# Hybrid decoder step: state updates by pairs of banks, scores on 32x32 blocks, sample updates behind their outputs

## The chip, the cores and the metric

The kernel runs on one core of a Trainium2 chip, written for the engines PE (TensorE), DVE (VectorE), ACT (ScalarE), POOL (GpSimd) and SP (which issues most DMAs). The metric is the device time of one execution in microseconds; smaller is better.

## The reference

The reference computes one step of a two-layer decoder for a prompt of 512 tokens and 8 samples of 8 tokens. In each layer half of the width is attention in three branches, and the other half a gated recurrence (HGRN2) with 4 heads and a 128 x 128 state per head, which is what the change is about. It is computed in chunks of 32 tokens for the prompt, and of 8 tokens for each sample:

```
a = where(causal, einsum('bnhcd,bnhsd->bnhcs', qe, ke), 0)   # scores within a chunk
o_intra = einsum('bnhcs,bnhse->bnhce', a, vh)
def step(S, inp):                                            # over the chunks
    qe_n, kd_n, v_n, dec_n = inp
    o_n = einsum('bhcd,bhde->bhce', qe_n, S)
    S = dec_n[..., None] * S + einsum('bhcd,bhce->bhde', kd_n, v_n)
    return S, o_n
o = rms_norm(o_intra + o_inter, out_gain) * sigmoid(g)
```

Everything is float32. All outputs of the layer feed one projection and an MLP.

## The kernel before

One program walks through the two layers. A layer has four parts: projections, then a block with the recurrence and the prompt's attention, then the compressed keys and the samples' attention, then output projection and MLP. Within a part each engine has its own list of instructions, written out by hand, and the engines wait for each other on semaphores. An engine works its list in order, so what stands behind a wait waits too. The order of the work around the change is the order of the calls at the end of each engine's function (L1332 to L1378 for PE, L1413 to L1457 for ACT, L1529 to L1575 for DVE).

The recurrence handles the prompt in four tiles t of 128 tokens, each of four chunks of 32, and the samples in two halves s of two heads. For a tile of the prompt:

- `scores` (L1171) makes the 128 x 128 scores of each head in bank 0 with four full products (L1178), though only the four 32 x 32 blocks on the diagonal are needed, and transposes the decayed keys into bank 1 (L1181). DVE's `masked` (L1466) copies what the mask lets through into `aTm`; the rest stays zero. ACT's `keep_kd` (L1381) copies the keys to `kdt`.
- `updates` (L1184) makes keys times values for the four chunks j into banks 4 to 7, one bank for a chunk, 32 rows of the array for each (L1191). It begins when the state update before it (`hg_state`) is done.
- `states` (L1479) is DVE's chain: for each chunk and head one instruction of 128 x 128 (L1489) computes the next state from the one before and the bank, 16 in all.
- `intra` (L1205) and `inter` (L1220) add scores times values and queries times states into bank 2 (bank 6 for the last tile). ACT's `keep_outputs` (L1388) norms the result into `on`, `turn_outputs` (L1250) transposes it into bank 3 (7), and DVE's `finish` (L1522) gates it.

The samples have `sample_outputs` (L1229, bank 3), `sample_updates` (L1195, again banks 4 to 7) and DVE's `sample_states` (L1496), which can overwrite the states only once the outputs are made; `select_samples` (L1506) takes the outputs from bank 3. `PROMPT` and `SAMPLES` number the six uses of banks 4 to 7: prompt 0, prompt 1, samples 0, prompt 2, samples 1, prompt 3.

Attention follows in the same block: `turn` (L1310) transposes queries and keys for it, through banks named in `TURN_BANKS`, and ACT copies them (L1429); `att_scores` (L1261) makes scores into banks 0 and 1, then 2 and 3, in turn (L1274), and DVE adds the mask and takes the maximum (L1561, L1563). The second `att_scores` uses banks 2 and 3 and waits for four of the finishes.

## Time and profile before

| | us |
|---|---|
| median of 3 runs | 1946.52 (1944.40 to 1946.86) |
| the profiled execution's own time | 1949.37 |
| its span, from first to last instruction | 1947.6 |
| PE, DVE, ACT, POOL busy in the span | 1862.8, 1139.6, 785.7, 665.2 |
| mean granted clock of PE | 0.985 |

In the rows further down, a line such as L1191 is that of this kernel. A product (matmul) of float32 appears as two records of PE, so x32 are 16 products. Shapes of PE are rows*columns of the weights and rows x columns of the moving operand. `HT`, `R`, `OT` and `RAW` are the large buffers of which all named tiles are cut.

### The profile page before, as it was taken

How to read it: one execution, taken by the hardware profiler on the slowest of the kernel's cores; microseconds unless marked ns; L12 is line 12 of the kernel's file. 1: busy time of each engine (PE TensorE's matmuls, PEld its weight loads, DVE VectorE, ACT ScalarE, POOL GpSimd, SP SyncE). 2: the span in 40 equal slices, each digit the busy share in tenths (PEclk: the TensorE clock that was granted, in tenths of full speed). 3: DMA queues.
4: the chain of work that ended last, by engine and by line, in shares of the span. 5: the costliest groups of instructions: out<-in, count | busy, mean ns of one | idle time of the engine just before them, and what ended most of it. 6: DMA issues, size and time to landing. Idle time of an engine off the chain costs nothing. (4 is left out here: it accounts for less than half of the span.)

```text
span 1947.6 us, 36998 instructions
## 1 busy us (share of the span) xinstructions
PE 1862.8 (96%) x15057; PEld 1720.0 (88%) x15057; DVE 1139.6 (59%) x1847; ACT 785.7 (40%) x1543; POOL 665.2 (34%) x452
## 2 busy tenths in 40 slices
PE   7999899999899999999999998999988999999999
PEld 6988567997799999999989875679968999999998
DVE  5588776555445454555537878756454455545554
ACT  4564375444433131313146635745444422323131
POOL 2432545230233333333323334544103333333331
PEclk8999999999999999999999998999999999999999
DMA  4221521325422222222222224222462222222221
GB/s 163 87 67 44 172 67 55 91 87 162 122 87 84 77 79 87 87 87 78 75 76 74 72 69 134 66 86 70 134 167 74 87 87 78 76 86 87 87 81 55
DMA packets 196053, 175.68 MB, mean 90 GB/s; under 512 B 11388, under 2 KB 189358, under 8 KB 195758
## 3 DMA queue, kind: packets, MB, share of 16 engines
q1 hardware_dynamic: 195778, 173.30, 29.2%
q8 instruction: 120, 1.97, 0.4%
q14 instruction: 47, 0.39, 0.1%
q10 hardware_dynamic: 108, 0.03, 0.0%
HBM read 162.67 MB, written 10.62 MB: 89 GB/s over the span
## 5 line engine op out<-in xcount | busy, mean ns | idle before, releaser
L389 POOL TENSOR_TENSOR WX<-RAW,WX 128x2048 fp32r<-128x2048 f32 (+1 forms) x46 | 210.7, 4581 | 357.6 <-ACT WX L385 357.6
L2661 DVE TENSOR_TENSOR sq<-sq 128x288 f32<-128x288 f32 x128 | 156.7, 1229 | 198.2 <-ACT sq L2626 198.2
L389 POOL TENSOR_TENSOR m_wl<-RAW,m_wh 128x2048 fp32r<-128x2048 f32 x36 | 165.1, 4587 | 308.5 <-ACT m_wh L385 308.5
L399 PE MATMUL bank<-UH,m_wh 128*128 128x288 f32 x640 | 188.9, 295 | 0.0
L401 PE MATMUL bank<-UH,m_wl 128*128 128x288 f32 x640 | 188.9, 295 | 0.0
L400 PE MATMUL bank<-UL,m_wh 128*128 128x288 f32 x640 | 188.7, 295 | 0.0
L401 PE MATMUL bank<-UH,WX 128*128 128x288 f32 x576 | 170.6, 296 | 0.0
L399 PE MATMUL bank<-UH,WX 128*128 128x288 f32 x576 | 170.6, 296 | 0.0
L400 PE MATMUL bank<-UL,WX 128*128 128x288 f32 x576 | 170.5, 296 | 0.0
L2680 DVE TENSOR_TENSOR OT<-bank,rstd 128x288 f32<-128x288 f32 x128 | 58.2, 454 | 186.3 <-PE bank L401 186.3
L2683 DVE TENSOR_TENSOR XT<-XT,OT 128x288 f32<-128x288 f32 x128 | 157.1, 1227 | 4.4
L1839 PE MATMUL bank<-FTS,W1S 128*128 128x256 f32 (+1 forms) x512 | 156.5, 306 | 0.0
L399 PE MATMUL bank<-m_ah,m_wh 128*128 128x288 f32 x512 | 151.3, 296 | 0.0
L401 PE MATMUL bank<-m_ah,m_wl 128*128 128x288 f32 x512 | 151.1, 295 | 0.0
L400 PE MATMUL bank<-m_al,m_wh 128*128 128x288 f32 x512 | 151.0, 295 | 0.0
L1842 PE MATMUL bank<-FTS,W1S 128*128 128x256 f32 (+1 forms) x512 | 150.7, 294 | 0.0
L1841 PE MATMUL bank<-FTS,W1S 128*128 128x256 f32 (+1 forms) x512 | 150.6, 294 | 0.0
L385 ACT ACTIVATE WX<-RAW 128x2048 fp32r<-128x2048 f32 (+1 forms) x46 | 86.4, 1878 | 157.3 <-PE bank L401 142.3
L2626 ACT ACTIVATE sq<-bank 128x288 f32<-128x288 f32 x128 | 52.5, 410 | 235.6 <-PE bank L401 218.9
L401 PE MATMUL bank<-m_ah,WX 128*128 128x288 f32 x448 | 132.7, 296 | 0.0
L400 PE MATMUL bank<-m_al,WX 128*128 128x288 f32 x448 | 132.6, 296 | 0.0
L399 PE MATMUL bank<-m_ah,WX 128*128 128x288 f32 x448 | 132.5, 296 | 0.0
(396 smaller groups left out, 5324.5 us busy)
## 6 DMA issues: line engine op xcount, KB each, us to landing
RAW<-in_w_up SPq DMA_DIRECT2D x32, 1024.0 KB, 5.4
RAW<-in_w_down SPq DMA_DIRECT2D x32, 1024.0 KB, 5.1
RAW<-in_w_in SPq DMA_DIRECT2D x20, 1024.0 KB, 5.0
R<-in_cache_nsa_kv SPq DMA_DIRECT2D x128, 64.0 KB
HT<-in_cache_nsa_kv SPq DMA_DIRECT2D x128, 64.0 KB, 2.7
RAW<-in_w_in SPq DMA_DIRECT2D x8, 792.0 KB, 4.5
R<-in_cache_nsa_kv SPq DMA_DIRECT2D x48, 128.0 KB, 2.3
out<-R SPq DMA_DIRECT2D x10, 512.0 KB, 4.6
```

What stands on the lines that cost most here:

```text
L385: act.activation(S.granule(S.wh, i, w), S.granule(S.raw, i, w), ACT.Copy).then_inc(sem(S.name + "w_hi"), 1)
L389: eng.tensor_tensor(S.granule(S.wl, i, w), S.granule(S.raw, i, w), S.granule(S.wh, i, w).bitcast(F32), ALU.subtract).then_inc(sem(S.name + ...
L399: pe.matmul(out, wh[:, c, cols], ah[:, c, n], start=(c == 0), stop=False)
L400: pe.matmul(out, wh[:, c, cols], al[:, c, n], start=False, stop=False)
L401: ins = pe.matmul(out, wl[:, c, cols], ah[:, c, n], start=False, stop=(c == KC - 1))
L1839: pe.matmul(out, W1H[:, s, c, cols], xh, start=first and (h == 0 or CU[w][1] == 0), stop=False, skip_group_check=True)
L1841: pe.matmul(out, W1H[:, s, c, cols], xl, start=False, stop=False, skip_group_check=True)
L1842: ins = pe.matmul(out, W1L[:, s, c, cols], xh, start=False, stop=last, skip_group_check=True)
L2626: act.activation(relu[n % 4], bank[2 + u % 6][:, 0:HALF], ACT.Relu).then_inc(sem("m_relued"), 1)
L2661: dve.tensor_tensor(relu[n % 4], relu[n % 4], relu[n % 4], ALU.mult).then_inc(sem("relu_squared"), 1)
L2680: dve.tensor_tensor(grown[n % 2], bank[2 + u % 6][:, 0:HALF], rstd[:, halves(s)], ALU.mult).then_inc(sem("m_added"), 1)
L2683: dve.tensor_tensor(x, x, grown[n % 2], ALU.add).then_inc(sem("m_grown"), 1)
```

## The change

Five edits, all in the block with the recurrence:

- `updates` and `sample_updates` are done by pairs of banks: the products for banks 4 and 5 first, when DVE has done the first half of the update before (`hg_chain`, or `hg_s_chain` for samples), and those for banks 6 and 7 when it has done all of it. `states` and `sample_states` wait for each pair apart.
- Scores of the prompt are made as 16 products of 32 x 32 (4 chunks, 4 heads), packed in 128 columns of bank 0; the mask, `aTm` and DVE's copy shrink to a quarter. `intra` takes them as 16 products of 32 rows by 32 columns, each from row group j into partitions 32j to 32j + 31 of the output bank.
- Sample updates come directly behind the sample outputs on PE, and DVE's sample states before the selection. The last state update comes ahead of `finish_samples`, and `finish(2)` and `turn_outputs(2)` come after attention's first score.
- The normed outputs have two buffers, so that ACT waits for the transposes of two tiles before.
- ACT norms the samples before it keeps the last keys, the turns begin behind the last updates, and the banks of the turns are swapped to fit.

The diff, each line with 12 spaces less at its start:

```diff
@@ -86,7 +86,7 @@
-put("hgmask", (i[:, None] // CH == i[None] // CH) & (i[:, None] <= i[None]))
+put("hgmask", i[:, None] % CH <= np.arange(CH)[None])
@@ -951,8 +951,9 @@
-aTm = [cut(HH * P).rearrange("p (h n) -> p h n", h=HH) for _ in range(2)]
-kdt, on = (cut(HH * P).rearrange("p (h e) -> p h e", h=HH) for _ in range(2))
...
+aTm = [cut(HH * CH).rearrange("p (h n) -> p h n", h=HH) for _ in range(2)]
+kdt, *on = (cut(HH * P).rearrange("p (h e) -> p h e", h=HH) for _ in range(3))
@@ -987,7 +988,7 @@
-TURN_BANKS = (0, 1, 0, 1, 2, 0, 1, 2)
+TURN_BANKS = (1, 0, 2, 1, 0, 2, 1, 2)
@@ -1175,32 +1176,49 @@
-                ins = pe.matmul(s[0:r, h * r:(h + 1) * r], hf[:, h, c], hq[:, h, c], start=True, stop=True)
+                if t == NT:
+                    ins = pe.matmul(s[0:r, h * r:(h + 1) * r], hf[:, h, c], hq[:, h, c], start=True, stop=True)
+                    continue
+                for j in range(NCK):
+                    x = slice(t * P + j * CH, t * P + (j + 1) * CH)
+                    ins = pe.matmul(s[j * CH:(j + 1) * CH, h * CH:(h + 1) * CH], hf[:, h, x], hq[:, h, x],
+                                    start=True, stop=True, skip_group_check=True)
...
+        def room(r, half):
...
+            if r == 0:
+                return
+            if half:
+                pe.wait_ge(sem("hg_state"), r)
+            elif r - 1 in PROMPT:
+                pe.wait_ge(sem("hg_chain"), HH * ((NCK - 1) * PROMPT.index(r - 1) + 2))
+            else:
+                pe.wait_ge(sem("hg_s_chain"), SAMPLES.index(r - 1) + 1)
...
         def updates(t):
-            if t:
-                pe.wait_ge(sem("hg_state"), PROMPT[t])
...
-            for h in range(HH):
-                for j in range(NCK):
-                    rr = slice(j * CH, (j + 1) * CH)
-                    ins = pe.matmul(bank[4 + j][:, h * P:(h + 1) * P], kdt[rr, h, :],
-                                    hi_tok[rr, t, h * P:(h + 1) * P], start=True, stop=True)
-            ins.then_inc(sem("hg_updates"), 1)
+            for half in range(2):
+                room(PROMPT[t], half)
+                for h in range(HH):
+                    for j in (2 * half, 2 * half + 1):
+                        rr = slice(j * CH, (j + 1) * CH)
+                        ins = pe.matmul(bank[4 + j][:, h * P:(h + 1) * P], kdt[rr, h, :],
+                                        hi_tok[rr, t, h * P:(h + 1) * P], start=True, stop=True)
+                ins.then_inc(sem("hg_updates"), 1)
         def sample_updates(s):
-            pe.wait_ge(sem("hg_state"), SAMPLES[s])
...
+                room(SAMPLES[s], h % 2)
...
-            ins.then_inc(sem("hg_updates"), 1)
+                ins.then_inc(sem("hg_updates"), 1)
         def intra(t):
@@ -1213,9 +1231,11 @@
-                pe.matmul(out_of(t)[:, h * P:(h + 1) * P], aTm[t % 2][:, h], hi_tok[:, t, h * P:(h + 1) * P],
-                          start=(h == 0), stop=False, skip_group_check=True)
+                for j in range(NCK):
+                    rr = slice(j * CH, (j + 1) * CH)
...
+                    pe.matmul(out_of(t)[rr, h * P:(h + 1) * P], aTm[t % 2][rr, h], hi_tok[rr, t, h * P:(h + 1) * P],
+                              start=(h == 0), stop=False, skip_group_check=True)
         def inter(t):
@@ -1255,7 +1275,7 @@
-                ins = pe.transpose(turned_of(t)[:, h * P:(h + 1) * P], on[:, h], ident)
+                ins = pe.transpose(turned_of(t)[:, h * P:(h + 1) * P], on[t % 2][:, h], ident)
...
         def att_scores(n):
@@ -1313,8 +1333,8 @@
-                pe.wait_ge(sem("hg_kd_kept" if u else "hg_masked"), NT)
-            elif u == 4:
+                pe.wait_ge(sem("hg_masked" if u else "hg_kd_kept"), NT)
+            elif u == 2:
@@ -1337,27 +1357,26 @@
         updates(1)
         inter(0)
         sample_outputs(0)
+        sample_updates(0)
         scores(2)
         intra(1)
-        sample_updates(0)
         inter(1)
         turn_outputs(0)
         updates(2)
         sample_outputs(1)
+        sample_updates(1)
         intra(2)
         scores(3)
+        inter(2)
         turn_outputs(1)
-        sample_updates(1)
-        inter(2)
+        updates(3)
+        turn(0)
+        turn(1)
         pe.wait_ge(sem("hg_s_normed"), 1)
         pe.wait_ge(sem("hg_finished"), 2)
         for s in range(2):
             ins = pe.transpose(bank[3][:, s * P:(s + 1) * P], s_out[s], ident)
         ins.then_inc(sem("hg_out_turned"), 1)
-        turn(0)
-        turn(1)
-        updates(3)
-        turn_outputs(2)
         for u in range(2, len(TURNS)):
             turn(u)
         for n in range(NA + LAG + 1):
@@ -1366,6 +1385,7 @@
             if n == 0:
                 intra(3)
                 inter(3)
+                turn_outputs(2)
             if n == 1:
                 for t in range(4):
                     turn_plain(t)
@@ -1382,22 +1402,22 @@
         def keep_kd(t):
...
-                act.wait_ge(sem("hg_updates"), PROMPT[t - 1] + 1)
+                act.wait_ge(sem("hg_updates"), 2 * PROMPT[t - 1] + 2)
...
         def keep_outputs(t):
...
-            if t:
...
-                act.wait_ge(sem("hg_out_turned"), t + (t == 3))
+            if t >= 2:
...
+                act.wait_ge(sem("hg_out_turned"), t - 1)
...
-                ins = act.activation(on[:, h], out_of(t)[:, h * P:(h + 1) * P], ACT.Square, accum_out=r[:, h:h + 1])
+                ins = act.activation(on[t % 2][:, h], out_of(t)[:, h * P:(h + 1) * P], ACT.Square, accum_out=r[:, h:h + 1])
...
-                ins = act.activation(on[:, h], out_of(t)[:, h * P:(h + 1) * P], ACT.Copy, scale=r[:, h:h + 1])
+                ins = act.activation(on[t % 2][:, h], out_of(t)[:, h * P:(h + 1) * P], ACT.Copy, scale=r[:, h:h + 1])
...
         def norm_samples():
@@ -1418,10 +1438,10 @@
         keep_outputs(0)
         keep_kd(2)
         keep_outputs(1)
+        norm_samples()
         keep_kd(3)
         act.activation(gate, win_tok[:, :, 256:WINW], ACT.Exp, scale=-1.0).then_inc(sem("gate_exp"), 1)
-        norm_samples()
         keep_outputs(2)
         for u, (k, t) in enumerate(TURNS):
             act.wait_ge(sem("turned"), u + 1)
@@ -1467,8 +1487,8 @@
-            dve.copy_predicated(aTm[t % 2], const("hgmask").bitcast(U32).unsqueeze(1).to_broadcast([P, HH, P]),
-                                bank[0].rearrange("p (h n) -> p h n", h=HH)).then_inc(sem("hg_masked"), 1)
+            dve.copy_predicated(aTm[t % 2], const("hgmask").bitcast(U32).unsqueeze(1).to_broadcast([P, HH, CH]),
+                                bank[0][:, 0:HH * CH].rearrange("p (h n) -> p h n", h=HH)).then_inc(sem("hg_masked"), 1)
         def sample_masked():
@@ -1477,9 +1497,10 @@
         def states(t):
-            dve.wait_ge(sem("hg_updates"), PROMPT[t] + 1)
...
+                if j % 2 == 0:
+                    dve.wait_ge(sem("hg_updates"), 2 * PROMPT[t] + 1 + j // 2)
@@ -1494,13 +1515,15 @@
         def sample_states(s):
-            dve.wait_ge(sem("hg_updates"), SAMPLES[s] + 1)
...
+                dve.wait_ge(sem("hg_updates"), 2 * SAMPLES[s] + 1 + h % 2)
...
+                if h % 2 == 0:
+                    ins.then_inc(sem("hg_s_chain"), 1)
...
         def select_samples(s):
@@ -1531,18 +1554,17 @@
         states(0)
         masked(1)
         states(1)
+        sample_states(0)
         select_samples(0)
         masked(2)
-        sample_states(0)
         finish(0)
         states(2)
         select_samples(1)
+        sample_states(1)
         masked(3)
         finish(1)
-        sample_states(1)
+        states(3)
         finish_samples()
-        states(3)
-        finish(2)
         dve.wait_ge(sem("gate_exp"), 1)
         step(dve, dve.tensor_scalar(gate, gate, 1.0, None, ALU.add), "dve_done")
         dve.reciprocal(gate, gate).then_inc(sem("gate_made"), 1)
@@ -1561,6 +1583,8 @@
+            if n == 0:
+                finish(2)
```

The order of PE, from the third tile's scores (before) to the second tile's inter. The names in brackets are semaphores: `hg_chain` counts DVE's single state instructions, `hg_state` whole updates. Before:

```order
L1178 MATMUL bank<-R_0 128x128 [waits hg_kd_kept_47,hg_masked_49]
L1178 MATMUL bank<-R_0 128x128 x3
L1181 MATMUL bank<-cst,R_0 128x128 x4
L1217 MATMUL bank<-R_0,HT 128x128 [waits hg_out_kept_55,hg_masked_49]
L1217 MATMUL bank<-R_0,HT 128x128 x3
L1202 MATMUL bank<-OT,R_0 128x512 [waits hg_apart_53,hg_s_kd_kept_52,hg_state_32]
L1202 MATMUL bank<-OT,R_0 128x512 x3
L1225 MATMUL bank<-R_0 32x128 [waits hg_state_32]
```

Now, L1220 being the sample updates, L1184 the scores and L1237 intra:

```order
L1220 MATMUL bank<-OT,R_0 128x512 [waits hg_chain_51,hg_apart_54,hg_s_kd_kept_53]
L1220 MATMUL bank<-OT,R_0 128x512
L1220 MATMUL bank<-OT,R_0 128x512 [waits hg_state_32]
L1220 MATMUL bank<-OT,R_0 128x512
L1184 MATMUL bank<-R_0 32x32 [waits hg_kd_kept_47,hg_masked_49]
L1184 MATMUL bank<-R_0 32x32 x15
L1188 MATMUL bank<-cst,R_0 128x128 x4
L1237 MATMUL bank<-R_0,HT 32x128 [waits hg_out_kept_56,hg_masked_49]
L1237 MATMUL bank<-R_0,HT 32x128 x15
L1245 MATMUL bank<-R_0 32x128 [waits hg_state_32]
```

The sample updates moved ahead of scores and intra, and were split in two, the first with a wait on half an update.

PE where attention begins, now (L1294 is an attention score, L1237 and L1245 the last intra and inter):

```order
L1294 MATMUL bank<-R_0 128x512 [waits turn_kept_63]
L1294 MATMUL bank<-R_0 128x512
L1237 MATMUL bank<-R_0,HT 32x128 [waits hg_state_32,hg_masked_49]
L1237 MATMUL bank<-R_0,HT 32x128 x15
L1245 MATMUL bank<-R_0 32x128 [waits hg_state_32]
L1245 MATMUL bank<-R_0 32x128 x15
L1278 MATMUL bank<-cst,HT 128x128 [waits hg_finished_59,hg_out_kept_56]
L1278 MATMUL bank<-cst,HT 128x128 x3
L1294 MATMUL bank<-R_0 128x512 [waits hg_finished_59,turn_kept_63]
```

The two L1278 rows, the transposes of the third tile's outputs, stood ahead of the third to the eighth turn before; they are now between the first and the second score.

## Rows read from the trace of the kernel before

**Rows 1.** The page, part 1: busy us, share of the span, instructions of each engine.
```profile
PE 1862.8 (96%) x15057; PEld 1720.0 (88%) x15057; DVE 1139.6 (59%) x1847; ACT 785.7 (40%) x1543; POOL 665.2 (34%) x452
```
**Rows 2.** DVE's waits, first block, then second: who waited for whom; us in all, times, longest.
```profile
DVE R L1489 <- PE bank L1191: 4.3, 4, 1.5
DVE R L1501 <- PE bank L1202: 3.0, 2, 1.9
...
DVE R L1489 <- PE bank L1191: 3.8, 4, 1.6
DVE R L1501 <- PE bank L1202: 2.0, 2, 1.2
DVE HT L1470 <- PE bank L1178: 1.7, 1, 1.7
```
**Rows 3.** Timeline of DVE, first block: start us, us, instructions, [idle before <-releaser].
```profile
202.39 4.22 DVE L1489 SCALAR_TENSOR_TENSOR R<-R,bank 128x128 f32<-128x128 f32 x16 [0.84 <-PE bank L1191]
...
206.65 0.74 DVE L1470 COPY_PREDICATED HT<-cst,bank 128x512 f32<-128x512 uint32 x1
...
213.07 1.12 DVE L1511 SCALAR_TENSOR_TENSOR rstd<-bank,cst,rstd 128x128 f32<-128x128 f32 x3
...
216.71 4.22 DVE L1501 SCALAR_TENSOR_TENSOR R<-R,bank 128x128 f32<-128x128 f32 x16 [1.87 <-PE bank L1202]
220.85 0.74 DVE L1526 SCALAR_TENSOR_TENSOR OT<-bank,par,R 128x512 f32<-128x512 f32 x1
...
231.65 4.22 DVE L1501 SCALAR_TENSOR_TENSOR R<-R,bank 128x128 f32<-128x128 f32 x16 [1.17 <-PE bank L1202]
```
**Rows 4.** Timeline of PE, first block.
```profile
198.49 1.13 PE L1178 MATMUL bank<-R 128*128 128x128 f32 x8 [1.03 <-PEq L609]
...
203.69 1.06 PE L1217 MATMUL bank<-R,HT 128*128 128x128 f32 x8
...
206.67 1.71 PE L1191 MATMUL bank<-R,HT 32*128 32x128 f32 x32 [1.93 <-DVE R L1489]
...
214.67 1.99 PE L1202 MATMUL bank<-OT,R 32*128 32x512 f32 x8
...
216.59 1.08 PE L1225 MATMUL bank<-R 128*32 128x128 f32 x32
...
220.98 2.09 PE L1191 MATMUL bank<-R,HT 32*128 32x128 f32 x32 [2.73 <-DVE R L1501]
...
235.92 1.17 PE L1191 MATMUL bank<-R,HT 32*128 32x128 f32 x32 [2.07 <-DVE R L1501]
```
**Rows 5.** Timeline, second block: DVE's last sample update, PE's second attention score.
```profile
1192.98 4.22 DVE L1501 SCALAR_TENSOR_TENSOR R<-R,bank 128x128 f32<-128x128 f32 x16 [1.17 <-PE bank L1202]
...
1205.19 1.13 PE L1274 MATMUL bank<-R 64*128 64x512 f32 x4
```
**Rows 6.** Timeline, from the recurrence to attention, first layer.
```profile
237.03 0.66 PE L1258 MATMUL bank<-cst,HT 128*128 128x128 f32 x4
...
238.16 2.77 ACT L1429 ACTIVATE R<-bank 128x512 f32<-128x512 f32 x6 [1.63 <-PE bank L1322]
...
243.86 1.13 PE L1274 MATMUL bank<-R 64*128 64x512 f32 x4
```
**Rows 7.** Windows: start:end, us, busy us of each engine (instructions), PEclk, DMA share, GB/s.
```profile
207.00:211.00 4.00, 4.00 (x72) 2.86 (x64) 2.96 (x11) 0.69 (x6) 3.69 (x7) 0.57 1.07 390
221.00:225.00 4.00, 4.00 (x42) 2.17 (x44) 2.45 (x9) 0.23 (x1) 3.53 (x6) 0.60 0.74 223
1180.00:1190.00 10.00, 9.59 (x62) 6.09 (x63) 6.64 (x23) 0.66 (x3) 5.32 (x8) 0.50 0.36 105
...
243.20:316.80 73.60, 71.57 (x650) 46.07 (x644) 57.99 (x135) 52.68 (x177) 38.26 (x64) 1.00 0.18 50
...
1204.50:1278.10 73.60, 71.57 (x650) 46.05 (x644) 57.99 (x135) 52.64 (x177) 38.27 (x64) 1.00 0.18 50
```
**Rows 8.** Timeline of PE, first layer: 16 products of 64 columns.
```profile
422.73 0.65 PE L1688 MATMUL bank<-R 128*32 128x64 f32 x32
```

## The prediction

> **What bounds the kernel now.** I read the page first: PE is busy 96% of the span [rows 1], so at first sight only PE's work matters. But a share is a mean over stages. The change touches one block of each layer, the one that starts at 198.5 us in the first layer and at 1159.5 us in the second, and there I asked for DVE's waits in both layers, then for the timeline of DVE and PE, then for the granted clock by windows.
>
> In that block DVE carries a chain of six updates: four of the prompt's state (16 instructions, 4.22 us each) and two of the samples' states (also 4.22 us). In front of every one DVE stands idle for PE, 4.3 us before the four and 3.0 before the two in the first layer [rows 2]. The reason is in the code: the four banks 4 to 7 that hold the new products are all released only when DVE has finished the whole update before, and then PE needs 1.1 to 2 us (L1191 and L1202, [rows 4]) in which DVE has only a mask or a finish to do. PE for its part was idle for DVE 1.93, 2.73 and 2.07 us before such products [rows 4]. In the second layer DVE's waits are 3.8 and 2.0, and 1.7 for a product that came late [rows 2]. The block is a chain DVE, PE, DVE, and neither engine bounds it alone.
>
> From the second attention score on, both layers take the same 73.6 us with the same busy times to 0.02 us (PE, DVE) [rows 7]. So whatever the block gives at that point is taken to go through to the end of the span. I measure each layer up to the second L1274, at 243.86 and 1205.19 us, that is 45.37 and 45.67 us after the block's start [rows 6, 5].
>
> **The change, part by part** (first layer, on its clock; PE at its higher level).
>
> *Start.* The scores become 16 products of 32 by 32. The nearest row is L1688, 16 products of 64 columns on 32 wide weights: 0.65 us against the 1.13 us of L1178 [rows 8, 4]. With the pair of banks ready after 1.0 us where all four took 1.17 [rows 4], the first state update begins at about 201.8 instead of 202.39: 0.6 us. The other scores lie beside DVE's updates and count nothing; under a missing cover they would save 0.5 us more each.
>
> *Masks.* 512 columns per partition take 0.74 us [rows 3]; 128 columns should take 0.35. Three later masks stand in the chain: 3 x 0.39 = 1.2 us. The smaller memsets at the start wait beside PE: nothing.
>
> *Updates by pairs.* A pair uses two 32-row groups at a time where all four worked before. L1202 runs so: four products of 512 columns in 1.99 us, so two rounds of 0.96 [rows 4]. A pair (eight of 128) costs the same 0.96 and two pairs 1.9, where 1.1 was enough. That is 0.8 us more of PE per update, but the first pair is computed under the second half of DVE's previous update (2.1 us), and the second under the first half of the next. The waits before the second update and before the last two (1.17 is one of these, [rows 3]) go to zero.
>
> *Samples behind their outputs.* After the first state update ends (206.06) PE runs one pair 0.95, inter 1.0, outputs 1.97, first sample pair 1.06: 211.1. DVE comes from its second update at 210.6 and waits 0.5. Its sample update ends at 215.3, the selection (1.43: 0.35 and the 1.12 of L1511, [rows 3]) and the mask bring it to 217.1. Behind the selection now hang the transposes of the first outputs, which PE must do before the third updates; DVE waits about 0.4 for them, finishes them in 0.74 [rows 3], and waits 0.2 for the pair. Third update to 222.5, selection to 223.95, second sample update without a wait: it ends at 228.15. Before, it ended at 231.65 + 4.22 = 235.87 [rows 3]. **7.7 us earlier.** In the second layer it ended at 1197.20, 37.7 after the start [rows 5] and so 0.3 later than in the first: 8.0.
>
> *End of the block.* From the second sample update's end PE has to do the last second pair (1.0), then eight groups of turns and the samples' transposes, with ACT's copies between them (0.5 each, 2.77 for six, [rows 6]): 4.1 us. Then the first attention score 1.05, intra 1.0, inter 1.0, the transposes of the third outputs 0.6, DVE's finish 0.74 with 0.1 of handing over: the second score starts 9.6 behind. The last finish is a **new wait**: it was done before attention began, and the second score needs it, since bank 3 is its target. Before, the distance was 243.86 - 235.87 = 8.0. So 1.6 us are given back. Two buffers for the normed outputs take ACT's wait for the transposes away; ACT is not late anywhere here: nothing.
>
> Sum at the higher clock: 7.7 - 1.6 = 6.1 in the first layer, 8.0 - 1.6 = 6.4 in the second, **12.5 us**.
>
> *The clock.* It was not at the higher level all the time. It was granted at 0.57 and 0.60 in two stretches of the first layer, and at 0.50 for 10 us in the second [rows 7], each beginning within about 2 us of an idle PE. Two levels, 1.0 and 0.5, make this 3.4 + 3.2 and 10 us at the lower, 16.6 in all. The sum above counts them all as gone. If the new order has as many, and PE is on its path in all of them, 16.6 x 0.5 = 8.3 us come back and 4.2 remain. By the same walk the new order has one idle stretch of PE of 2 us (before the first transposes) and some below 0.7, where the old one had three of about 2 or more in each layer [rows 4]. I take about half of the low time: 12.5 - 4.2 = 8.3, rounded to **8 us**, which is nearer to what the missing idle stretches say than either end.
>
> *Intra on blocks.* 16 products of 32 rows by 32 columns replace four full ones, L1217, 1.06 us [rows 4]. The nearest rows are L1225, 16 products in four column groups that write one bank in 1.08 us, and L1191, 16 in four row groups that write four banks in 1.17. If a diagonal block uses its group of rows and of columns alone, four run at once and the cost stays 1.0: taken so, no change. But no row has different row groups writing the same bank. One after the other they would be four times as long, 4 us. That is the other bound, and it is large.
>
> The Trainium skill, "TensorEngine Tiling (Array Packing)", section Restrictions and Gotchas, speaks against this edit: different row tiles cannot access the same PSUM bank simultaneously. With it the sum would be that of the second rival below; by the column-group row it is the 8 us above. No row of this trace shows which holds for a diagonal.
>
> Sum for the profiled execution: 1949.4 - 8 = 1941.4 us (its span 1947.6 to 1939.6). It lies 2.9 above the median of the runs; I take the same difference off the median: 1946.5 - 8 = **1938.5 us**.
>
> **The rivals.**
> 1. *The chain shortens, the clock is no better.* For: PE's work is now cut into smaller pieces and a low stretch did not need a long idle (one of 1.93 us went before it in the first layer, the same in the second had none). Against: fewer idle stretches. Price: 8.3 of the 12.5 given back, 1942.3 us.
> 2. *Slower: intra's blocks run one after another.* Place: the four L1217 of a layer. Each costs 3 us more. The first delays the second updates by 2.4 beyond what the states cover, the second and third hold up the transposes that DVE waits for, 1.2 and about 2, the fourth stands in full between the first and second score, 3: some 9 us a layer against 6.2 gained. 2 x (9 - 6.2) = +6: 1952.5 us. It decides from about 2.3 us more per product, a block of 3.3 us. Against: row groups and column groups each run together in this trace.
> 3. *The gain is absorbed in front of attention.* The second score's new wait grows: if ACT's keep of the third outputs or its eight copies are 2 us later than I have them, turns, first score and finish all move with them, and 2 x 2 us go; with some low clock that leaves 2 to 3 us: 1944 us. For: ACT is busy from the third outputs to the last copy nearly without a gap. Against: its outputs start 1 us before the last state update does.
>
> **How the numbers follow.** A measurement of this kernel tells about 0.2% (3.9 us) from no change. Forecast with a clock between half as bad and clean: 0.60. Rival 1: 0.20, half of it just over the bound and half under. Rival 2: 0.12, most of it slower, the rest about even where the blocks overlap in part. Rival 3: 0.08, no difference. Faster: 0.60 + 0.10 and a part of the others, 0.74; same 0.16; slower 0.10. The range reaches from the clean clock, 1946.5 - 12.5 = 1934, to 1945, which takes in rivals 1 and 3 and leaves out rival 2 and a little on each side.
>
> **What would show it.** Right: DVE's idle time before the updates falls from 7.3 us to about 2.2 in the first layer, the first of about 1.1 included; the second L1274 comes 39 to 42 us after the start of the block; PE waits there for DVE's finish; intra stays near 1.0 us at the full clock. Windows of 0.5 in the block, as long as before, would mean rival 1. Intra of 3 to 4 us would mean rival 2. Attention longer than 73.6 us, or a clock lower elsewhere, would make the assumption wrong that the block's gain reaches the end.

## The result: slower by 6.4 us, with a lower clock of PE in the block

| | before | after |
|---|---|---|
| median of 7 runs each, us | 1946.52 (1944.40 to 1949.11) | 1952.93 (1951.97 to 1955.60) |
| ratio, with its 95% interval | | 1.0037 (1.0025 to 1.0049) |
| span of the profiled execution, us | 1947.6 | 1952.5 |
| mean granted clock of PE in it | 0.985 | 0.982 |
| first block: start of scores to second attention score, us | 45.37 | 48.23 |
| second block | 45.67 | 46.80 |
| PE at its lower clock level, in the first and the second block, us | 6.8 and 10.2 | 17.1 and 13.7 |

The forecast was 8 us faster. The two blocks became 4.0 us longer together and the span 4.9. The other 0.9 us lie outside the blocks, where the time at the lower clock was about the same (41 us before, 40 after); their cause is not known. In the rows of after, L1209 are the prompt's updates, L1220 the samples', L1237 intra, L1245 inter, L1261 and L1266 the sample outputs, L1278 the transposes of the normed outputs, L1294 attention's scores.

The page of after, part 1, against [rows 1]:

```profile
PE 1870.1 (96%) x15441; PEld 1720.2 (88%) x15441; DVE 1133.0 (58%) x1847; ACT 786.8 (40%) x1543; POOL 665.0 (34%) x452
```

DVE works 6.6 us less, as the smaller masks promised. PE is busy 7.3 us longer although its scores shrank: the same products took longer. DVE's waits in the first block, against [rows 2]:

```profile
DVE OT L1549 <- PE bank L1278: 4.3, 2, 3.2
DVE R L1510 <- PE bank L1209: 2.8, 3, 1.3
DVE R L1522 <- PE bank L1220: 2.7, 2, 2.2
```

Of the 7.3 us before the six updates 5.5 are left, 2.2 of them before the first samples' update alone, and 4.3 us in front of the two finishes are new. The timeline of PE in that block says why, against [rows 4]:

```profile
206.86 1.16 PE L1209 MATMUL bank<-R,HT 32*128 32x128 f32 x16 [0.69 <-DVE R L1510]
...
210.08 1.20 PE L1261 MATMUL bank<-R 128*32 128x512 f32 x8 [1.05 <-DMA R<-in_state_hgrn]
...
212.21 1.99 PE L1220 MATMUL bank<-OT,R 32*128 32x512 f32 x8
...
215.10 1.08 PE L1237 MATMUL bank<-R,HT 32*32 32x128 f32 x32
216.11 1.08 PE L1245 MATMUL bank<-R 128*32 128x128 f32 x32
219.28 1.07 PE L1278 MATMUL bank<-cst,HT 128*128 128x128 f32 x4 [2.08 <-DVE rstd L1534]
220.28 3.10 PE L1209 MATMUL bank<-R,HT 32*128 32x128 f32 x32
223.31 1.94 PE L1261 MATMUL bank<-R 128*32 128x512 f32 x8
225.18 1.97 PE L1266 MATMUL bank<-OT,R 64*64 64x512 f32 x4
227.08 3.78 PE L1220 MATMUL bank<-OT,R 32*128 32x512 f32 x8
230.79 1.93 PE L1237 MATMUL bank<-R,HT 32*32 32x128 f32 x32
...
247.47 1.09 PE L1294 MATMUL bank<-R 64*128 64x512 f32 x3 [0.93 <-DVE OT L1549]
```

Three things are to be seen. Intra on blocks (L1237) takes 1.08 us at the full clock, so the second rival's mechanism is not there. PE waits 1.05 us for the samples' states, a DMA: their outputs now come early enough to meet it. And PE stands 2.08 us in front of the first output transposes, for the selection (L1534), which DVE now does behind the first samples' state update; from there on the larger products take nearly double, 3.78 us where L1220 had 1.99, 1.93 where L1237 had 1.08. The windows of after, with the columns of [rows 7]:

```profile
219.30:236.30 17.00, 17.00 (x157) 9.25 (x158) 10.86 (x39) 3.52 (x15) 5.86 (x9) 0.50 0.31 84
1184.60:1198.20 13.60, 13.60 (x121) 6.83 (x122) 10.57 (x38) 2.74 (x12) 5.69 (x9) 0.52 0.27 82
```

PE shows no idle time in these 17 us, at 0.50, the lower of its two levels. The second layer repeats it, with the wait for the DMA 1.25 and the idle stretch 2.08 us:

```profile
1175.53 1.07 PE L1261 MATMUL bank<-R 128*32 128x512 f32 x8 [1.25 <-DMA R<-in_state_hgrn]
...
1184.60 0.63 PE L1278 MATMUL bank<-cst,HT 128*128 128x128 f32 x4 [2.08 <-DVE rstd L1534]
1185.15 3.03 PE L1209 MATMUL bank<-R,HT 32*128 32x128 f32 x32
...
1211.28 1.13 PE L1294 MATMUL bank<-R 64*128 64x512 f32 x4 [0.94 <-DVE OT L1549]
```

So there were three suspects: the idle stretch; the products, many of which now fill a small part of the array; and the states' DMA.

### The profile page after: what moved, and what is told of

Same layout as the page of the kernel before. It is cut to its first block and busy times, and to the rows that moved or that the text cites. A ratio compares the mean times of both kernels' runs of the same rounds, so it can differ in the third digit from the quotient of the medians.

```text
span 1952.5 us, 37770 instructions
## 1 busy us (share of the span) xinstructions
PE 1870.1 (96%) x15441; PEld 1720.2 (88%) x15441; DVE 1133.0 (58%) x1847; ACT 786.8 (40%) x1543; POOL 665.0 (34%) x452
```

## The experiments

Low time is summed over windows of 1 us as (1 - clock) x 2 x length, for the two blocks of the profiled execution. A profile is one execution of 5 to 12, and low stretches move from one to the next, so the last column has the mean granted clock of all executions; 0.001 of it is 3.9 us of low time. Before had 0.9858 to 0.9862 in the four sittings (17 to 31 executions each) and a median of 1945.94 to 1946.86 us. Behind after, four rows of the table at a time are one sitting, on a chip of its own with before beside it. After was measured only ahead of them, so every difference to after is one between sittings; the ratio to before is the safer figure. Short names stand for the kernels.

| kernel | median us | ratio to before (95%) | blocks us | low time us | clock |
|---|---|---|---|---|---|
| after | 1952.93 | 1.0037 (1.0025 to 1.0049) | 48.23, 46.80 | 17.1, 13.7 | 0.9817 |
| warm | 1948.07 | 1.0009 (0.9998 to 1.0021) | 42.44, 42.42 | 3.4, 3.4 | 0.9858 |
| unsplit | 1951.54 | 1.0027 (1.0013 to 1.0041) | 47.78, 45.52 | 17.1, 10.2 | 0.9828 |
| more work | 1943.33 | 0.9985 (0.9972 to 0.9998) | 45.28, 43.75 | 6.8, 3.4 | 0.9876 |
| updates first | 1944.66 | 0.9987 (0.9976 to 0.9998) | 43.88, 44.52 | 6.8, 10.2 | 0.9863 |
| states' loads first | 1950.86 | 1.0019 (1.0006 to 1.0031) | 46.54, 42.10 | 13.7, 3.4 | 0.9822 |
| before, warm | 1952.57 | 1.0028 (1.0017 to 1.0040) | 44.00, 44.67 | 6.8, 6.8 | 0.9866 |
| three edits | 1943.70 | 0.9984 (0.9975 to 0.9994) | 42.24, 43.86 | 0.0, 3.4 | 0.9878 |
| before, blocks only | 1949.56 | 1.0021 (1.0011 to 1.0031) | 44.42, 44.48 | 10.2, 6.8 | 0.9828 |
| states apart | 1947.64 | 1.0013 (1.0001 to 1.0024) | 40.85, 42.10 | 3.4, 3.4 | 0.9831 |
| select first, states apart | 1938.68 | 0.9963 (0.9950 to 0.9975) | 39.44, 39.51 | 0.0, 3.4 | 0.9878 |
| select, more work | 1945.42 | 0.9986 (0.9971 to 1.0001) | 44.15, 41.15 | 6.8, 3.4 | 0.9863 |
| updates, more work | 1945.35 | 0.9994 (0.9984 to 1.0003) | 46.92, 40.80 | 13.7, 0.0 | 0.9868 |
| select, full size | 1939.51 | 0.9964 (0.9951 to 0.9977) | 40.39, 40.38 | 0.0, 0.0 | 0.9882 |
| select, unsplit | 1949.32 | 1.0012 (1.0001 to 1.0023) | 44.90, 46.53 | 10.2, 13.7 | 0.9834 |
| select first alone | 1939.13 | 0.9961 (0.9948 to 0.9974) | 39.69, 39.88 | 0.0, 3.4 | 0.9872 |
| select, apart, again | 1939.02 | 0.9965 (0.9952 to 0.9979) | 40.77, 38.51 | 3.4, 0.0 | 0.9865 |

**The idle stretch filled: warm.** Two full products of 512 columns that nobody reads stand in it.

```diff
                     inter(1)
+                    warm(3, 2)
                     turn_outputs(0)
```

> Edit: in the changed kernel, two extra full products of 512 columns (into bank 1, unused there) stand on PE ahead of the transposes of the first outputs, where PE had idled 2.08 us in both layers, just before its clock fell. Nothing else is changed. Idle theory (the fall comes from the idle stretch): no stretch at 0.5 in the block, which is then 40.7 us long in the first layer (my walk with the wait for the samples' states) instead of 48.2, and 40.9 instead of 46.8: 13 us less, about 1940 us. Density theory (the fall comes from products that fill only half of the array's rows for twice as long): the clock falls all the same when the extra products are over, within 5 us; total 1949 to 1953 us.

Measured: 1948.07 us. The idle stretch fell to 0.17 us, the blocks to 42.4 us and their low time from 30.8 to 6.8. The block behaved as the idle theory has it. The median fell by 4.9 us and the profiled execution, the fastest of ten, by 8.8 (1954.56 to 1945.77); the mean clock is that of before.

**Pairs undone: unsplit.** All four banks behind one wait, in `updates` and likewise in `sample_updates`.

```diff
-                        for half in range(2):
-                            room(PROMPT[t], half)
-                            for h in range(HH):
-                                for j in (2 * half, 2 * half + 1):
+                        room(PROMPT[t], 1)
+                        for h in range(HH):
+                            for j in range(NCK):
...
-                            ins.then_inc(sem("hg_updates"), 1)
+                        ins.then_inc(sem("hg_updates"), 2)
```

> Edit: in the changed kernel the updates are again made for all four banks at once, after the whole state update before; order, blocks of scores and buffers stay as changed. Density theory: with four row groups at work at once, the low stretch becomes much shorter (under 5 us a layer) or does not come; the waits of DVE for PE return (5 x 1.2 us a layer) but the clock's 13.4 us go, total 1946 to 1951. Idle theory: PE idles more (before each of six updates about 2 us), so the low stretches stay as long as now or grow: 1955 to 1962 us.

Measured: 1951.54 us, low time 27.3 us, with 2.9 us of idle PE in front of the first transposes. The low clock is there without the pairs. In this order they seemed to be worth nothing; that reading was reversed later.

**More work.** Three full score products per tile, overwritten by the small ones behind them.

```diff
+                        if t < NT:
+                            for h in range(1, HH):
+                                pe.matmul(s[:, h * P:(h + 1) * P], hf[:, h, c], hq[:, h, c], start=True, stop=True)
```

> Edit: in the changed kernel, ahead of the 16 small score products of each tile stand three full products of 128 x 128 whose results nobody reads, so that a tile's scores cost PE about what they cost before (0.75 us more) and use the array fully. Density theory by way of the small scores: the low stretch shortens by at least half, total 1944 to 1948 us. Idle theory: the idle 2 us before the transposes remain, and so does the fall; each extra product costs a little: 1953 to 1957 us.

Measured: 1943.33 us, 9.6 less than after with more work to do. This looked like proof that the small products cost the clock. But the added products also fill the idle stretch: PE had no wait for the selection in the first block and 1.2 us in the second. The edit moves both suspects, and its result tells neither from the other.

**Updates first.** The third updates go ahead of the first transposes on PE, so that PE has work there.

```diff
-                    turn_outputs(0)
                     updates(2)
+                    turn_outputs(0)
```

> Edit: in the changed kernel, one pair of calls on PE swaps places: the third updates come before the transposes of the first outputs, so that PE works on them in the time in which it idled 2.08 us; the idle time is cut into two pieces of at most 1.0 us. No extra work. Idle theory: no fall at that place, block of 40 to 41 us, total 1939 to 1943 us. Density theory: the clock falls as before at 219 us, total within 2 us of 1953.

Measured: 1944.66 us, 8.3 less than after with the same products. PE's waits in the part that was slow in after are 0.85 us at most, but the blocks, 43.88 and 44.52 us with 17.0 us of low time, are longer than the 40 to 41 expected, and the time misses 1939 to 1943. In both layers the clock fell 5 us later in the block than in after, at the second samples' updates, behind a wait of 0.85 us.

**The states' loads ahead of everything else on their queue.**

```diff
                                      ).then_inc(sem("s0_loaded"), 16)
+                    sp.wait_ge(sem("s0_loaded"), 16 * HH)
```

> The kernel after, with one wait added: the queue that loads the samples' states waits until all four are there before it issues the transfers behind them (stores, and a load of 2 MB of weights for the MLP). In the kernel after, PE waited 1.05 and 1.25 us for these states in front of the sample outputs, and DVE 2.2 us before the first samples' state update. Theory: the states compete with the transfers behind them. Then PE's wait for R<-in_state_hgrn falls to under 0.3 us in both layers, and at equal low clock each block is 1.5 to 1.7 us shorter: 1952.9 - 3 = 1950 us. Rival: the states are limited by their own latency; then the wait stays near 1 us and the time within 1 us of the kernel after. Low clock of PE can move either way by 3.4 us a layer, which is 1.7 us of time each.

Measured: 1950.86 us. The two layers disagree. PE's wait in the first block is what it was; in the second there is none. PE's waits in the first block, then its timeline at the same outputs in the second:

```profile
PE bank L1279 <- DVE rstd L1535: 2.1, 1, 2.1
...
PE bank L1262 <- DMA R<-in_state_hgrn: 1.0, 1, 1.0
```

```profile
1172.94 1.94 PE L1262 MATMUL bank<-R 128*32 128x512 f32 x8
```

With the loads untouched the wait also comes and goes: 0.37 and 0.76 us in warm, none and 0.38 in more work, 1.15 and 0.34 in select first alone. So this run does not show whether the transfers behind delay the states.

**Fillers in the kernel before.**

```diff
+                    warm(2, 2)
                     updates(1)
...
                     turn_outputs(0)
+                    warm(3, 3)
                     updates(2)
```

> The kernel before, with idle time of PE filled: two full products of 512 columns ahead of the second tile's updates and three ahead of the third tile's, where PE waited 1.9 and 2.7 us for DVE. Nothing else changes. Theory that PE's idle stretches in this block cost the clock: low time, 6.8 and 10.2 us in the kernel before, falls to 3.4 or less a layer, and the time by about half of 10 us less what the filler adds to the path (up to 1 us a layer): 1946.4 - 3 = 1943 us. Rival, that the low clock follows how little of the array PE's products fill in this block, and full products help because they fill it: the same sign here, so this run alone does not tell them apart; if neither holds, low time stays at 17 us and the time rises by 0 to 2 us.

Measured: 1952.57 us, against 1943 expected, a miss. The blocks did get shorter, by 1.4 and 1.0 us, and the mean clock did not fall; the first block's gain was gone again at 513 us. Part of what is lost elsewhere can be seen: PE stands still for 11.4 us in all without a wait that the profile shows ("issue"), against 6.9 us in before, the most of all kernels here. Two of these stops, each inside a row of equal products, set PE back by 1.7 and 2.1 us against before:

```profile
512.14 0.32 PE L2318 MATMUL bank<-R,R2s 64*32 64x64 f32 x8 [1.40 <-issue]
...
1475.20 0.25 PE L2318 MATMUL bank<-R,R2s 128*32 128x64 f32 x2 [1.74 <-issue]
```

The edit touches nothing there; it only adds instructions to PE's list ahead of them, and why the stops grow is not known. The 4.5 us are about half of what is missing, so this run tells little about fillers as such.

**Three edits at once** (more work, updates first, states' loads first).

> The kernel after with three edits at once: three full score products of 128 by 128 a tile ahead of the small ones, the third tile's updates ahead of the first transposes on PE, and the samples' states loaded before the transfers behind them. Each of the first two brought low time down from 30.8 us in both layers (to 10.2 and 17.1) and the time by 9.6 and 8.3 us. If they add, low time is 3.4 us a layer or less and the blocks are 40 to 41 us long, against 45.4 and 45.7 before: 1946.4 - 9 = 1937 us. If both remove the same low time, the blocks stay at 42 to 44 us and the time at 1941 to 1943 us.

Measured: 1943.70 us. They do not add: the second reading of the expectation.

**The blocks of 32 alone, in the kernel before.**

> The kernel before, with only the scores, the mask and intra on blocks of 32 by 32; order, banks and buffers as before. DVE's chain is shorter by 0.5 us at the start and 1.2 us in masks, 1.7 us a layer. Theory that it is the missing full products of the scores that cost the clock: low time rises from 6.8 and 10.2 us to 13 or more a layer, and the time is 1946.4 - 3.4 + 0.5 x 10 = 1948 us or more. Rival, that idle time alone sets the clock, and this hardly changes here: low time as before, 1943 us.

Measured: 1949.56 us, slower by 3.2 where DVE's chain is shorter. The mean clock fell from 0.9862 to 0.9828, although the low time of the two blocks in the profile is before's, 17.0 us, so the profile does not show where it fell. But here too smaller work makes PE's waits longer (2.4 and 2.7 us before the updates and 1.2 before a transpose, where before had 1.9 and 2.7 and 1.0), so this does not separate size from idle time either.

**States apart.** The first two heads' states count on a semaphore of their own.

```diff
-                                     ).then_inc(sem("s0_loaded"), 16)
+                                     ).then_inc(sem(f"s0_loaded{h // 2}"), 16)
...
-                        pe.wait_ge(sem("s0_loaded"), 16 * HH)
+                        pe.wait_ge(sem(f"s0_loaded{s}"), 32)
```

> The kernel after, with one edit: the samples' states of the first two heads and of the last two count on semaphores of their own, so that the first sample outputs no longer wait for all four loads (2 MB). Holding back the transfers behind them left PE's wait at 1.0 us, and the four loads took 7 us at the 290 to 330 GB/s that the trace shows, so it is the loads' own bytes that PE waits for. The first two of them land about 3 us before the last. Theory: PE's wait for R<-in_state_hgrn is gone in both layers, and at equal low clock a block is 1.3 us shorter: 1952.9 - 2.6 = 1950.3 us, up to 3.4 us either way by the clock. Rival: another wait ends last there (the samples' decayed keys, or DVE's mask), and PE stands at the sample outputs still.

Measured: 1947.64 us. The wait for the DMA is gone, the idle stretch stays at 2.09 us, and the mean clock stays low at 0.9831: single executions lay between 1945.1 and 1952.7. The profiled one was the fastest, with low time of only 3.4 us a block. In its second block these 3.4 us lie ahead of the idle stretch, at 1166.0, and behind the stretch the clock stays high:

```profile
1177.29 0.63 PE L1278 MATMUL bank<-cst,HT 128*128 128x128 f32 x4 [2.08 <-DVE rstd L1534]
```

```profile
1177.30:1194.30 17.00, 15.95 (x224) 10.88 (x224) 15.87 (x57) 9.63 (x35) 5.56 (x9) 1.00 0.42 115
```

Three kernels have this stretch of 2.08 or 2.09 us in both layers (after, states' loads first, states apart). Of their six stretches four were followed within 1.2 us by low time, of 17.1, 13.7, 13.7 and 3.4 us, and two by none; in these two a low stretch of 3.4 us had come some 11 us ahead.

**Select first, states apart.** Two lines of DVE's list change places.

```diff
+                    select_samples(0)
                     sample_states(0)
-                    select_samples(0)
```

> The one before it in this list (states apart), and on DVE the first selection goes ahead of the first sample states, which it fills a wait with; ACT then norms the samples, and PE gets its first output transposes, about 4 us earlier, so that the idle stretch of 2.08 us goes without a move of any work of PE. Theory that this idle stretch starts the long low time: low time falls from 17.1 and 13.7 us to 7 or less a layer, the blocks to 42 us, and the time to 1945 us or less. Rival, that the low time follows from how little of the array is used in these 20 us whatever the idle time: low time stays over 10 us a layer and the time at 1948 to 1950 us.

Measured: 1938.68 us, 14.3 less than after and 7.3 less than before on its chip. No work of PE moved against states apart.

**Select, more work, and updates, more work**: select first, states apart, with full score products added in tiles 1 to 3; and updates first with the same products and with the states apart.

> The one before it (states apart, selection first), with three full score products of 128 by 128 in addition in the tiles 1 to 3, ahead of the small ones. If idle time and small products both count, low time is 3.4 us a layer or none, the blocks are 40 to 41 us long, and the time is 1946.4 - 9 = 1937 us. If the idle time alone counts, it is that of the run before it plus up to 1 us.

> The kernel of three edits at once, with the samples' states on two semaphores in place of the wait of the queue, and no added products in tile 0. The block of that kernel had 1.35 us of idle time of DVE before the first sample states, and 1.22 us before the first state update; both should shrink, to 0.3 and 0.8. Blocks 40.5 and 41.5 us against 42.24 and 43.86, and 1943.7 - 3.5 = 1940 us. If the clock takes it back (low time 3.4 us more a layer), 1943 us.

Measured: 1945.42 and 1945.35 us. Neither reached its forecast. The first is 6.7 us slower than without the added work, and its executions fall into two groups, 1936 to 1937 and 1942 to 1947. More products of full size are no cure in themselves.

**Which part is worth what, in the good order.** The last four ran on one chip. Full size undoes the second edit of the change and, for room, the second buffer of the normed outputs; unsplit has the diff shown above; select first alone is after with the two lines of DVE exchanged and nothing else; the last is select first, states apart, once more.

```diff
+                            ins = pe.matmul(s[0:r, h * r:(h + 1) * r], hf[:, h, c], hq[:, h, c], start=True, stop=True)
...
+                            pe.matmul(out_of(t)[:, h * P:(h + 1) * P], aTm[t % 2][:, h], hi_tok[:, t, h * P:(h + 1) * P],
+                                      start=(h == 0), stop=False, skip_group_check=True)
...
-            kdt, *on = (cut(HH * P).rearrange("p (h e) -> p h e", h=HH) for _ in range(3))
+            kdt, *on = (cut(HH * P).rearrange("p (h e) -> p h e", h=HH) for _ in range(2))
+            on = on * 2
```

> The kernel of 1938.7 us (states apart, selection first) with the change's second edit undone: scores as full 128 by 128 products, the mask over 512 columns, intra in four full products. The masks take the room of one buffer, so the normed outputs have one again. At the full clock a block gets 0.5 us longer at the start and 0.4 to 1.2 by the masks: +1.5 us a layer, 1941.7 us. Theory that the small products lower the clock (the kernel before with only the blocks of 32 showed 13.5 us more low time in the mean of its executions): the mean low time falls under the 47 us of the kernel this one is made from, by up to 10, and gives 2 to 5 us back: 1938 us. Rival, that once the idle stretch is gone the products' size does not matter: low time the same, 1941 to 1942 us.

> The same kernel of 1938.7 us with the change's first edit undone: products for all four banks at once, when DVE has finished the update before. By the steps of the prediction each of three later updates a layer begins 0.9 to 1.2 us later: +3 us a layer, 1944.7 us at the same clock. Theory that the pairs are worth what the prediction says: 1943 us or more. Rival, that order and selection carry the gain and the pairs are hidden behind the samples' updates: within 1 us of 1938.7. In the kernel after, undoing the pairs changed nothing (1951.5 against 1952.9).

> The kernel after with the selection first on DVE and nothing else: the samples' states stay on one semaphore, so PE's wait of 1.05 and 1.25 us for them stays too. States apart alone gave 1947.6 us (5.3 less than after, of which at most 3 at equal clock), both together 1938.7. Theory that the idle stretch of 2.08 us before the first output transposes starts the low time, and the wait for the samples' states adds only its length: 1938.7 + 2.6 = 1941.3 us. Rival, that any idle stretch over about 1 us in this part does it, this one too: low time 10 us or more a layer, 1947 us.

> The kernel of 1938.7 us once more, for its interval and as the base of the three ahead of it on the same chip: 1938.7 us within 1 us, blocks of 39.5 us when neither has a low stretch and 41 with one. If the low result came of six lucky executions it will be nearer 1942.

Measured: full size 1939.51, unsplit 1949.32, select alone 1939.13 (1941.3 or 1947 expected), the base again 1939.02 us. Timeline of PE in select first alone, the same place as in after:

```profile
210.09 1.07 PE L1261 MATMUL bank<-R 128*32 128x512 f32 x8 [1.15 <-DMA R<-in_state_hgrn]
...
215.99 1.08 PE L1245 MATMUL bank<-R 128*32 128x128 f32 x32
217.00 0.66 PE L1278 MATMUL bank<-cst,HT 128*128 128x128 f32 x4
217.59 1.72 PE L1209 MATMUL bank<-R,HT 32*128 32x128 f32 x32
219.24 1.06 PE L1261 MATMUL bank<-R 128*32 128x512 f32 x8
220.23 1.08 PE L1266 MATMUL bank<-OT,R 64*64 64x512 f32 x4
```

Up to L1245 it is the timeline of after within 0.12 us, the wait for the DMA included. Then the transposes come without a wait, and the clock stays where it was. DVE's timeline and its waits there, and the windows:

```profile
212.28 0.35 DVE L1532 TENSOR_SCALAR rstd<-bank,cst 128x128 f32<-128x128 f32 x1 [1.10 <-PE bank L1266]
212.67 1.12 DVE L1534 SCALAR_TENSOR_TENSOR rstd<-bank,cst,rstd 128x128 f32<-128x128 f32 x3
213.71 4.22 DVE L1522 SCALAR_TENSOR_TENSOR R<-R,bank 128x128 f32<-128x128 f32 x16
```

```profile
DVE R L1510 <- PE bank L1209: 1.2, 1, 1.2
DVE rstd L1532 <- PE bank L1266: 1.1, 1, 1.1
DVE OT L1549 <- PE bank L1278: 0.9, 1, 0.9
```

```profile
217.00:234.00 17.00, 15.95 (x228) 10.89 (x224) 16.81 (x61) 11.54 (x45) 7.91 (x12) 1.00 0.53 151
1170.00:1187.00 17.00, 16.29 (x266) 10.95 (x255) 16.11 (x58) 9.33 (x41) 10.13 (x15) 0.90 0.63 189
```

The selection fills most of the 2.2 us in which DVE waited for the samples' products; the samples' state update starts 0.22 us later than in after (213.71 against 213.49). In 17 us DVE does 16.8 us of work where it did 10.9 in the low stretch of after. Only the first update of the prompt still waits for PE, as forecast.

In unsplit PE and DVE wait for each other again, DVE 7.0 us before the updates, PE for DVE up to 2.5 us at a time, with 10.2 and 13.7 us of low time behind:

```profile
PE bank L1219 <- DVE R L1509: 2.9, 2, 2.4
PE bank L1208 <- DVE R L1509: 2.5, 1, 2.5
...
PE bank L1208 <- DVE R L1521: 0.9, 1, 0.9
```

**What the runs settle.** (1) The place of the selection on DVE made the change slow: moving it back ahead of the samples' states, alone, takes 13.8 us off after (1952.93 to 1939.13; 14.8 by the ratios, 1.0037 and 0.9961), while products, pairs and the loads stay. In the profiles the blocks lose 15.5 us: 27.4 us less low time is 13.7 of it by the half, and 1.8 are left for the idle time itself. (2) The pairs are worth 10.3 us where nothing else stalls the chain (1949.32 against 1939.02), and looked worthless where something did. Most of that is clock again: the mean clock differs by 0.0031, 12 us of low time, about 6 of the 10.3. In the profiles the blocks differ by 12.2 us and their low time by 20.5; with half of it taken off, 1.9 us are left of the 6 that the steps of the prediction give. (3) The blocks of 32 are worth nothing that is measured: 1939.51 without them, 1939.02 with. Blocks without low time are 1 to 2 us shorter with them (38.51 and 39.44 against 40.38 and 40.39), and a mean clock lower by 0.0017, 6.6 us of low time, gives about that back. (4) The wait for the states' DMA, 1.15 and 0.34 us in the profile, costs nothing that is measured in the good order: 1939.13 with it, 1939.02 without. In the order of after its removal went with 5.3 us less (1952.93 to 1947.64; 4.7 by the ratios), more than the 2.3 us of its length.

**What stays open.** What exactly sends the clock down. Filling the idle stretch in three different ways, by fillers, by other work, by an earlier release, cut the low time in the blocks each time, from 30.8 us to between 3.4 and 17.0 us; but in "updates, more work" 13.7 us of low time followed idle stretches of 1.1 us at most, and two of six stretches of 2.08 us were followed by none. So the stretch makes long low time likely here, and does not set it alone. Whether the small products bear a share of it is not separated: "full size" has the higher mean clock (0.9882 against 0.9865, 5 and 6 executions), within the scatter between two sittings of its base (0.9878 and 0.9865).

## Why the prediction was wrong

- **The sum at the higher clock held.** Forecast: 6.1 and 6.4 us off the blocks, so 39.3 us each. Taking half of the low time off the blocks of after gives 48.23 - 8.55 = 39.7 and 46.80 - 6.85 = 39.95; select first alone had 39.69 us in a block without low time, and the base 38.51. In that block of select first alone the second sample update ends 29.5 us after the start (forecast 29.7), and the second score starts 10.1 us behind it (9.6). The blocks of after are 0.4 and 0.7 us over the forecast by this count; the wait for the DMA, below, is a part of it.
- **The clock term failed**, and by itself it turned the sign. The step was: one idle stretch of 2 us where the old order had three, so "about half of the low time", 8.3 of 16.6 us, a cost of 4.2. The trace of after has 30.8 us, a cost of 15.4: 11.2 us more, which turns 8 faster into 3 slower. The prediction counted idle stretches and ignored what stands behind each. Behind this one stood all of the third updates, both sample products and intra, on the path: DVE waited up to 3.2 us for the transposes at the end of them, and the low time ran on for 17 us. The text even named the stretch (2 us before the first transposes) and put no price on it.
- **The first rival** had the right sign of mechanism and the wrong size: "as long as before" was its worst case, 16.6 us. No case had more low time than before, and none of the range's ends covered it.
- **An uncosted wait**: the samples' outputs moved toward their DMA. The four loads were issued at 199.2 us and the last landed near 210, and PE came at 209.0. The prediction moved the outputs to a transfer it had not looked up. It is 1.05 and 1.25 us of PE in the trace, more than the 0.4 and 0.7 us that the blocks of after are over the forecast once the clock is taken off.
- **Masks, updates, turns**: DVE's busy time fell by 6.6 us, of which eight masks are 8 x 0.44 = 3.5. A mask takes 0.30 us (forecast 0.35), the small scores 0.46 (0.65), two pairs 1.72 when PE doesn't wait between them (1.9). The new wait of the second attention score for the finish is there, 0.93 and 0.94 us.
- **The second rival** was wrong in its mechanism and gave, by chance, the measured time (1952.5). Intra on the diagonal took 1.08 us: different row groups wrote one bank side by side. The Trainium skill, "TensorEngine Tiling (Array Packing)", section Restrictions and Gotchas, states that different row tiles cannot access the same PSUM bank simultaneously. The rows of L1237 decide against it here.
- **The third rival** did not occur: the distance from the first to the second attention score was 4.7 us in both layers (forecast 4.5), and in the first layer the same products of attention stand 72.8 us behind the second score, before and after. The 73.6 us of [rows 7] are windows that begin 0.7 us ahead of that score; the reading that the layers are alike holds.

## What to carry over

When a chain between two engines is tightened, list for each wait that remains who is released late and what is queued behind it; a short helper (here 1.5 us of selection) goes where its engine waits anyway, ahead of the long step, not behind it. Let the worst case for a remaining idle stretch of PE be the work that follows it at half speed, and let the range reach to more low time than before, not only to as much. And judge a part of a change in the order in which nothing else stalls: the pairs looked worthless in the bad order and were worth 10 us in the good one, most of it by the clock.

## What was not expected of the hardware

- PE stayed at its lower level for 17.0 us in which the profile shows no gap (219.30 to 236.30 us). Most of its products there fill parts of the array.
- The time spent at either level differs between executions of one kernel: select, more work had executions of 1936.2 us at a mean clock of 0.990 and of 1947.1 us at 0.985.
- PE stops for up to 2.5 us at a time without a wait that the profile shows: 6.4 to 11.4 us in all, the most in before, warm.
- Sixteen products of 32 x 32 weights with 128 columns, four row groups into one bank, take 1.08 us, as long as four full ones (1.06).
